# One-hot operands laid out token by token, and key numbers picked in bf16, in a two-layer encoder with product-key experts

## What is computed

```
def one(x):                                   # x: 128 tokens of RMSNorm(x)
    q = (x @ wq).reshape(C, 8 heads, 2, 128)
    s = einsum('chpk,hpnk->chpn', q, sub_keys)           # scores of 128 keys, two halves
    top_s, top_i = top_k(s, 16)
    cand = top_s[:, :, 0, :, None] + top_s[:, :, 1, None, :]
    best_s, best_j = top_k(cand.reshape(C, 8, 256), 16)
    i1 = take_along_axis(top_i[:, :, 0], best_j // 16)   # key number of the first half
    i2 = take_along_axis(top_i[:, :, 1], best_j % 16)    # key number of the second half
    e = i1 * 128 + i2
    g = softmax(best_s)
    h = gelu(einsum('cd,chkd->chk', x, expert_u[e]))
    return einsum('chk,chkd->cd', g * h, expert_v[e])
```

## Time and profile before

| | us |
|---|---|
| median of 3 runs | 3570.25 |
| the runs | 3565.03, 3570.25, 4163.93 |
| the profiled execution, its own time | 3574.14 |
| span of the profiled execution | 3572.3 |
| mean granted clock of PE, share of full | 0.972 |

### The profile page before, as it was taken

How to read it: one execution, slowest core, us unless ns; L and a number is a source line. 1 busy time by engine, 2 the same in 40 slices (tenths; PEclk the granted TensorE clock), 3 DMA queues, 4 the chain that set the end, 5 groups by cost and what they waited for, 6 DMA issues and landing times.

```text
span 3572.3 us, 55663 instructions
## 1 busy us (share of the span) xinstructions
PE 3347.4 (94%) x17714; PEld 2967.7 (83%) x17714; DVE 2547.1 (71%) x4795; ACT 1246.7 (35%) x2013; POOL 1161.9 (33%) x647
## 2 busy tenths in 40 slices
PE   7999998699879999999999999986998799999999
PEld 6787798699868888888877878886998688888888
DVE  4544699888688676676645547998886877676676
ACT  4433332233333333333344423222332333333332
POOL 3444344101233333333144443441112333333331
PEclk9999999899989999999999999998999899999999
DMA  3111343477788888888521123435677888888885
GB/s 120 65 53 65 107 132 110 165 260 269 283 304 318 310 302 307 304 297 304 202 101 65 53 77 110 126 115 178 247 273 282 303 319 306 309 300 303 298 305 205
DMA packets 235870, 763.87 MB, mean 214 GB/s; under 512 B 19056, under 2 KB 117488, under 8 KB 200688
## 3 DMA queue, kind: packets, MB, share of 16 engines
q1 hardware_dynamic: 198896, 494.09, 39.7%
q0 software_dynamic: 36864, 268.45, 21.8%
HBM read 684.87 MB, written 77.59 MB: 213 GB/s over the span
## 4 chain that ended last, share of the span: by engine, by line
PE 67%; DVE 15%; DVEq 6%; issue 6%; DMA 3%; ACT 1%; POOL 1%; SPq 0%; ACTq 0%; POOLq 0%
PE PS L417 19%; PE PS L419 19%; PE PS L418 19%; PE PS L691 6%; DVE EQ L1268 2%; PE PS L584 1%; DVEq L1277 1%; DVEq L1315 1%; DVE I L1221 1%; DVE I L1228 1%; DMA VRAW<-in_peer_v 1%; DVE SW L1222 1%; POOL RL L1418 1%; PE PS L578 1%; DVE EQ L1272 1%
## 5 line engine op out<-in xcount | busy, mean ns | idle before, releaser
L1418 POOL TENSOR_TENSOR RL<-RAW,RH 128x1024 fp32r<-128x1024 f32 x320 | 801.8, 2515 | 824.2 <-ACT RH L763 823.9
L417 PE MATMUL PS<-XH,RH 128*128 128x384 f32 (+1 forms) x2720 | 985.5, 362 | 21.6 <-ACT GEL L950 21.6
L419 PE MATMUL PS<-XH,RL 128*128 128x384 f32 (+1 forms) x2720 | 957.8, 352 | 0.0
L418 PE MATMUL PS<-XL,RH 128*128 128x384 f32 (+1 forms) x2720 | 956.5, 352 | 0.0
L1452 POOL DMA_INDIRECT ROWS<-in_peer_rows,LIST x256 | 292.0, 1141 | 1449.2 <-DVE X L1316 1405.2
L417 PE MATMUL PS<-VHI,WHI 128*128 128x512 f32 x1536 | 601.9, 392 | 40.9 <-DVE WLO L1375 40.9
L419 PE MATMUL PS<-VHI,WLO 128*128 128x512 f32 x1536 | 600.1, 391 | 0.0
L418 PE MATMUL PS<-VLO,WHI 128*128 128x512 f32 x1536 | 600.1, 391 | 0.0
L1372 DVE TENSOR_TENSOR VLO<-VRAW,VHI 128x1024 fp32r<-128x1024 f32 x256 | 321.6, 1256 | 340.2 <-ACT VHI L958 340.2
L417 PEld LDWEIGHTS PS<-XH,RH 128*128 128x128 f32 x2720 | 520.8, 191 | 50.9 <-issue 22.9
L418 PEld LDWEIGHTS PS<-XL,RH 128*128 128x128 f32 x2720 | 518.6, 191 | 28.3
(11 more groups left out here) (228 smaller groups left out, 3454.3 us busy)
## 6 DMA issues: line engine op xcount, KB each, us to landing
RAW<-in_peer_u SPq DMA_DIRECT2D x256, 512.0 KB, 5.6
VRAW<-in_peer_v SPq DMA_DIRECT2D x256, 512.0 KB, 5.6
RAW<-in_stream SPq DMA_DIRECT2D x128, 512.0 KB, 3.3
route_dram<-STAGE SPq DMA_DIRECT2D x16, 3072.0 KB, 10.1
GC<-route_dram SPq DMA_DIRECT2D x64, 768.0 KB, 8.7
gelu_dram<-GS SPq DMA_DIRECT2D x128, 192.0 KB, 3.6
GB<-gelu_dram SPq DMA_DIRECT2D x32, 768.0 KB, 10.0
ROWS<-in_peer_rows,LIST POOLq DMA_INDIRECT x256, 6.9
```

The source lines that it names most:

```text
L417: pe.matmul(acc, sh, mh, start=first, stop=False)
L418: pe.matmul(acc, sh, ml, start=False, stop=False)
L419: return pe.matmul(acc, sl, mh, start=False, stop=last)
L1418: pool.tensor_tensor(RL[:, k % 4, :], RAW[:, k % 2, :], RH[:, k % 4, :].bitcast(F32), ALU.subtract).then_inc(S.low_part, 1)
```

## The change

Picking the key numbers: F16, JF, J8 and the compare table EQ become bf16, with the token tile innermost (4 adjacent values). One compare of 2048 elements takes the place of the eight, one product of 2048 the place of the two, and four sums of halves (1024, 512, 256 and 128 outputs, the last one in float32 to I12) that of the two reductions, with a drain after each. The casts at lines 1246 and 1255 now write with the token tile innermost. Every value is a whole number under 128.

One-hot operands: OA, OE and OB become [8 tokens, 128], so a one-hot vector is contiguous. IT holds each value twice, and the operands are written as [8, 64, 2], with the pair from IT read again 64 times. They are still five operations of 1024 elements. REST, OA and OE move to other addresses.

```
-        IOTA4 = sb("IOTA4", [P, P, 4], BF16)
+        IOTA4 = sb("IOTA4", [P, TOPK, TT], BF16)
+        IOTAB = sb("IOTAB", [P, P], BF16)
-        EQ = at("EQ", 22 * K, [P, TT, TOPK, TOPK])
-        EQ2 = at("EQ2", 26 * K, [P, TT, TOPK, TOPK])
+        EQ = at("EQ", 22 * K, [P, 2, TOPK, TOPK, TT], BF16)
+        EQS = at("EQS", 26 * K, [P, 2, TOPK, 8, TT], BF16)
-        F16 = at("F16", 31 * K, [P, TT, 2, TOPK])
+        F16 = at("F16", 31 * K, [P, 2, TOPK, TT], BF16)
-        JF = at("JF", 32 * K + 512, [P, 2, TT, TOPK])
-        J8 = at("J8", 42 * K, [P, TT, TOPK])
+        JF = at("JF", 32 * K + 512, [P, 2, TOPK, TT], BF16)
+        J8 = at("J8", 42 * K, [P, TOPK, TT], BF16)
+        I12 = at("I12", 38 * K, [P, 2, TT, P])
-        IT = at("IT", 48 * K, [P, 5, SD], BF16)
+        IT = at("IT", 48 * K, [P, 5, SD, 2], BF16)
-        OA = at("OA", 55 * K, [P, 2, 2, P, 4], BF16)
-        OE = at("OE", 59 * K, [P, 2, P, 4], BF16)
-        OB = at("OB", 61 * K, [P, 2, 3, 2, P, 4], BF16)
+        OA = at("OA", 56 * K, [P, 2, 8, P], BF16)
+        OE = at("OE", 73 * K, [P, 8, P], BF16)
+        OB = at("OB", 61 * K, [P, 2, 3, 8, P], BF16)
...
-                                    m = pe.matmul(PS[:, 4 + g % 2, t * P:(t + 1) * P], OA[:, g // 2 % 2, g % 2, :, t],
-                                                  OB[:, g // 2 % 2, p, g % 2, :, t], start=p == 0, stop=p == 2)
+                                    m = pe.matmul(PS[:, 4 + g % 2, t * P:(t + 1) * P], OA[:, g // 2 % 2, g % 2 * 4 + t, :],
+                                                  OB[:, g // 2 % 2, p, g % 2 * 4 + t, :], start=p == 0, stop=p == 2)
...
-                        dve.tensor_copy(F16[:], I16[:])
+                        dve.tensor_copy(F16[:].rearrange("p h r t -> p t h r"), I16[:])
...
-                        dve.tensor_copy(JF[:], JHL[:])
+                        dve.tensor_copy(JF[:].rearrange("p h j t -> p h t j"), JHL[:])
...
-                        ramp = IOTA[:, 0:TOPK].unsqueeze(1).to_broadcast([P, TOPK, TOPK])
-                        for half, (e, dst) in enumerate(((EQ, I1), (EQ2, I2))):
-                            for t in range(TT):
-                                dve.tensor_tensor(e[:, t], JF[:, half, t, :].unsqueeze(2).to_broadcast([P, TOPK, TOPK]),
-                                                  ramp, ALU.is_equal)
+                        rows = EQ[:].rearrange("p h j r t -> p (h j) r t")
+                        dve.tensor_tensor(rows, JF[:].rearrange("p h j t -> p (h j) t").unsqueeze(2).to_broadcast(
+                            [P, 2 * TOPK, TOPK, TT]), IOTA4[:].unsqueeze(1).to_broadcast([P, 2 * TOPK, TOPK, TT]),
+                            ALU.is_equal)
                         dve.drain()
-                        for half, e in enumerate((EQ, EQ2)):
-                            dve.tensor_tensor(e[:], e[:], F16[:, :, half, :].unsqueeze(2).to_broadcast([P, TT, TOPK, TOPK]),
-                                              ALU.mult)
+                        flat = EQ[:].rearrange("p h j r t -> p h j (r t)")
+                        dve.tensor_tensor(flat, flat, F16[:].rearrange("p h r t -> p h (r t)").unsqueeze(2).to_broadcast(
+                            [P, 2, TOPK, TOPK * TT]), ALU.mult)
                         dve.drain()
-                        for e, dst in ((EQ, I1), (EQ2, I2)):
-                            dve.tensor_reduce(dst[:, :, bass.ds((2 * i + head) * TOPK, TOPK)], e[:], AX, ALU.add)
+                        sums = EQS[:].rearrange("p h j r t -> p (h j) r t")
+                        dve.tensor_tensor(sums, rows[:, :, 0:8, :], rows[:, :, 8:16, :], ALU.add)
+                        dve.drain()
+                        for n in (4, 2):
+                            dve.tensor_tensor(sums[:, :, 0:n, :], sums[:, :, 0:n, :], sums[:, :, n:2 * n, :], ALU.add)
+                            dve.drain()
+                        dve.tensor_tensor(I12[:, :, :, bass.ds((2 * i + head) * TOPK, TOPK)].rearrange("p h t j -> p h j t"),
+                                          EQS[:, :, :, 0, :], EQS[:, :, :, 1, :], ALU.add)
                         dve.drain()
...
-                    dve.tensor_copy(IT[:, n, :] if n < 2 else REST[:, 0, :], PS[:, n, 0:SD])
+                    if n < 2:
+                        dve.tensor_copy(IT[:, n], PS[:, n, 0:SD].unsqueeze(2).to_broadcast([P, SD, 2]))
+                    else:
+                        dve.tensor_copy(REST[:, 0, :], PS[:, n, 0:SD])
...
-                    dve.tensor_copy(IT[:, 2 + p, :], REST[:, p % 2, :])
+                    dve.tensor_copy(IT[:, 2 + p], REST[:, p % 2, :].unsqueeze(2).to_broadcast([P, SD, 2]))
...
-                            return IT[:, row, bass.ds(8 * n, 8)].rearrange("p (g t) -> p g t", g=2).unsqueeze(
-                                2).to_broadcast([P, 2, P, 4])
-
-                        numbers = IOTA4[:].unsqueeze(1).to_broadcast([P, 2, P, 4])
+                            return IT[:, row, bass.ds(8 * n, 8), :].unsqueeze(2).to_broadcast([P, 8, P // 2, 2])
+
+                        def tokens(tile):
+
+                            return tile.rearrange("p t (i d) -> p t i d", d=2)
+
+                        numbers = IOTAB[:].rearrange("p (i d) -> p i d", d=2).unsqueeze(1).to_broadcast([P, 8, P // 2, 2])
-                        dve.tensor_tensor(OA[:, slot], numbers, of_tokens(0), ALU.is_equal)
-                        dve.tensor_tensor(OE[:], numbers, of_tokens(1), ALU.is_equal)
+                        dve.tensor_tensor(tokens(OA[:, slot]), numbers, of_tokens(0), ALU.is_equal)
+                        dve.tensor_tensor(tokens(OE[:]), numbers, of_tokens(1), ALU.is_equal)
                         dve.drain()
                         for p in range(3):
-                            m = dve.tensor_tensor(OB[:, slot, p], OE[:], of_tokens(2 + p), ALU.mult)
+                            m = dve.tensor_tensor(tokens(OB[:, slot, p]), tokens(OE[:]), of_tokens(2 + p), ALU.mult)
```

More of the change, by code:

```diff
@@ L204, in program @@
         BS = at("BS", 37 * K, [P, TT * PH])
-        I1 = at("I1", 38 * K, [P, TT, P])
-        I2 = at("I2", 40 * K, [P, TT, P])
+        I12 = at("I12", 38 * K, [P, 2, TT, P])
+        I1, I2 = I12[:, 0], I12[:, 1]
         STAGE = [at(f"STAGE{s}", 24 * K * s, [P, NK, TB]) for s in range(2)]
-        IT = at("IT", 48 * K, [P, 5, SD], BF16)
-        REST = at("REST", 52 * K, [P, 2, SD])
-        OA = at("OA", 55 * K, [P, 2, 2, P, 4], BF16)
-        OE = at("OE", 59 * K, [P, 2, P, 4], BF16)
-        OB = at("OB", 61 * K, [P, 2, 3, 2, P, 4], BF16)
+        IT = at("IT", 48 * K, [P, 5, SD, 2], BF16)
+        REST = at("REST", 75 * K, [P, 2, SD])
+        OA = at("OA", 56 * K, [P, 2, 8, P], BF16)
+        OE = at("OE", 73 * K, [P, 8, P], BF16)
+        OB = at("OB", 61 * K, [P, 2, 3, 8, P], BF16)
         VRAW = at("VRAW", 0, [P, 2, D])
@@ L1000, in _ @@
             dve.wait_ge(iota_made, 1)
-            dve.tensor_copy(IOTA4[:], IOTA[:].unsqueeze(2).to_broadcast([P, P, 4]))
+            dve.tensor_copy(IOTA4[:], IOTA[:, 0:TOPK].unsqueeze(2).to_broadcast([P, TOPK, TT]))
+            dve.tensor_copy(IOTAB[:], IOTA[:])
             dve.wait_ge(const_in, 64)
@@ L1293, in _ @@
                     dve.wait_ge(S.choice_transposed, count(l, "choice_transposed", n + 1))
-                    dve.tensor_copy(IT[:, n, :] if n < 2 else REST[:, 0, :], PS[:, n, 0:SD])
+                    if n < 2:
+                        dve.tensor_copy(IT[:, n], PS[:, n, 0:SD].unsqueeze(2).to_broadcast([P, SD, 2]))
+                    else:
+                        dve.tensor_copy(REST[:, 0, :], PS[:, n, 0:SD])
                 dve.drain()
                 for p in range(3):
-                    dve.tensor_copy(IT[:, 2 + p, :], REST[:, p % 2, :])
+                    dve.tensor_copy(IT[:, 2 + p], REST[:, p % 2, :].unsqueeze(2).to_broadcast([P, SD, 2]))
                     dve.drain()
                     if p < 2:
-                        dve.tensor_tensor(REST[:, (p + 1) % 2, :], REST[:, p % 2, :], IT[:, 2 + p, :], ALU.subtract)
+                        dve.tensor_tensor(REST[:, (p + 1) % 2, :], REST[:, p % 2, :], IT[:, 2 + p, :, 0], ALU.subtract)
                         dve.drain()
```

## The result

The changed kernel takes 3509.4 us (median of 4 runs, 3508.6 to 3510.4) against 3570.4 for the kernel before, a ratio of 0.983 (95% interval 0.981 to 0.984): 61 us less. The forecast was 3527, in a range of 3494 to 3560. The profiled execution took 3508.56 us with a span of 3506.7, against 3572.3. One run of the kernel before, at 4163.93 us, was slow and is left out of the ratio.

The account below looks back on a forecast made before the run. DVE was taken to bound the query stage, with routing balanced between DVE and PE. 3574.1 - 46 (pick) + 3 (turn) = 3531 us profiled; the runs' median lies 3.9 lower, so 3527, range 3494 to 3560.

Parts of the forecast that it names:

- What bounds the query stage: Query stage: DVE leads at 32.5 us per head, becoming 29.6, a hair above PE's 29.5.
- PE's wait at the end of the stage: Query stage end: 27 us minus what DVE gains, some 23 us in a layer, so it hides nothing.
- The pick, 2.9 us per head: Query stage, DVE, undisturbed: 7.9 us removed, 4.7 added, 0.3 for small edits; 16 heads give 46 us.
- small edits: Pick: casts to F16 and JF and the last sum write with jumps, 0.1 us each taken, 0.3 per head.
- Collisions, left at nothing with 18 us either way: Pick: POOL low parts stall two-input DVE instructions; 4 us saving left out, 2.2 us in every other head as range.
- Turn, +3 us: Between query and routing stages: IT twice as wide lengthens copies and casts, 1.4 us per layer, 3 us in all.
- DVE's one-hot operations at 687 ns: Routing stage: five instructions of 1024 bf16 elements keep their time though the inner run shrinks from four values to two.
- the rival: Routing stage: one-hot operands lose the paired rate, 1225 ns instead of 687, +240 us, 3767 us; chance 0.11.
- the estimate was 3680 us: Routing stage: by the skill page's rule on hopping at every word, one-hot instructions cost +0.35 us each.
- I take contiguity to bring PE nothing: Routing stage, PE: the weight load sets 108 ns per pair, and contiguous one-hot vectors leave it unchanged.
- the first rival: Routing stage: PE loads contiguous one-hot vectors faster, DVE then binds, 17 us gained, 3510 us; chance 0.27.
- 1.07 us of gaps that it counted as slack: Routing stage, DVE: three longer gaps, 0.17 + 0.20 + 0.70 us over the usual, put DVE's own pace at 33.7 us per round.

Follow-up runs that it names:

- both experiments on collisions: Changed kernel with two reductions replacing the pick's four sums: 3498.0 us; changed kernel with POOL writing 8 of 1024 columns per query-stage low part: 3489.7 us.
- the reductions: Changed kernel with the pick's four sums of halves replaced by two reductions over the 16 ranks: 3498.0 us, ratio 0.979.

## Why the prediction was right or wrong

- **What bounds the query stage** (DVE, down to PE's 29.5 us per head): right. DVE leads in the changed kernel's chain, and both experiments on collisions ran into PE. What it says of PE's wait at the end of the stage (27 us minus what DVE gains) was wrong: by the 27 us gained nothing would have been left, and 15.11 us were. It took PE's own end of the stage as fixed, but PE had lost 10 us in waits for DVE within the stage and ended 13.5 us earlier. That the margin held is luck: by the prediction's own sum it would have been used up.
- **The pick, 2.9 us per head:** right for the untouched part: 4.7 us, small edits 0.1 each.
- **Collisions, left at nothing with 18 us either way:** mis-sized, by 10 us. By mean against undisturbed time the pick lost 54 us before (Rows 3, 4) and loses 37 after, 33 at L1277 and 4 at L1273. The steps ahead of the pick lost about 25 us before and 32 after (L1243 16 x (0.83 - 0.23) = 10, L1263 16 x (1.22 - 0.19) = 16, two others 6). Two of those before, at 226 and 219 ns undisturbed:

```profile
L1256 DVE TENSOR_TENSOR BV<-B 128x64 f32 x16 | 8.0, 500 | 0.0
L1246 DVE CAST F<-I 128x128 f32<-128x128 uint32 x16 | 7.9, 493 | 0.0
```

So 79 us became 69, and 46 + 10 is the 57 measured, to within 1. All 16 heads have a collision at L1277, 12 at L1243, 8 at L1263. Before, the most that one place had was 17 of the 128 compares and 8 of the 32 products: they had offered POOL several places. The period of DVE's heads and that of PE's blocks, on which ACT's and POOL's parts follow, are now 29.4 and 29.5 us, so each head meets POOL at the same place. That it is this lock is argued from the times. With the reductions, which don't stand still, the collisions went to L1263 (10 of 16 heads), L1245 (7) and L1248 (5), at an unchanged 29.4 us per head, which fits it; no run shifted POOL's work against DVE's and left the rest alone.
- **Turn, +3 us:** +2.1. The copies cost what was priced, 0.395 and 0.20 us each, 1.4 us in a layer; a third of a microsecond of it fell into a wait for PE's transposes.
- **DVE's one-hot operations at 687 ns:** right, and the rival had a true mechanism at a run of one. The rule of the Trainium skill ("Vector Engine (DVE) Microarchitecture Reference", 5.2) against runs of one 4-byte word, by which the estimate was 3680 us, didn't show here, where the word is read again in place: 687 ns. What its section 5.1 has, that rows of two 16-bit elements still run paired, did.
- **"I take contiguity to bring PE nothing": this step failed.** The runs showed in its place that the hops of the moving operand set the pace: 108 ns per pair at 8 bytes, 53 contiguous. The inference that the load sets it, from 0.11 against 0.15 us per pair at 96 and 128 weight columns, rests on a misreading. The row of 0.59 us in Rows 11 begins with a load that went ahead while a product of 512 columns was still streaming. By the matmuls of the same two groups, in the kernel before, there is no difference:

```profile
157.47 0.60 PE L578 MATMUL PS<-IDN,PR 128*128 128x128 f32 x4
```

```profile
164.85 0.60 PE L548 MATMUL PS<-IDN,QSL 128*96 128x128 f32 x4
```

Less the last one's 0.27 us both are 0.33 / 3 = 0.11 us per pair. The contiguous load of 114 ns that I set beside OA's 108 was float32, and no run says which operand sets the pace there, so it said nothing of a bf16 stream. The rule that I quoted from the Trainium skill ("SBUF — State Buffer", "Door 1: The DMA port swizzle"), that two hits on a line of 16 bytes are enough for full speed, has two on a line at 8 bytes. The pace there was 108 ns, so for the moving operand it is refuted; the 54 ns came with 4 bytes. Nor was the weight path slow, which the Trainium skill ("TensorE: Matmul & The Clock Gate", "Weight-path perf modes") has fast for such weights: with OA hopping 8 bytes and OB contiguous a pair took 54 ns.
- **What the first rival was worth:** its 17 us came out as 14.8. It said DVE's pace would bind, and it does; but of the 1.07 us of gaps that it counted as slack only the one of 0.92 was a wait for ACT. The others are DVE's own, and a round went from 34.8 to 34.3, not 33.7. By the starts of OA, the first seven rounds of both layers gained 9.2 us. Behind the last OB of a layer PE now starts its last one-hot product after 3.1 us instead of 6.3 and 6.1, since it no longer runs behind DVE: 6.2 us more. With 0.6 lost on the way to WF that is the 14.8. The 17 us were thus near by luck: the slack was counted too large and the end of the stage not at all.

So the time came 18 us under the forecast: 11 from the query stage, 15 from routing, 1 from the turn, less the 4 of the rest and 5 of the profiled executions' places among their runs' medians. It stayed within the range because the lower end had been drawn from just these two, the first rival's 3510 and fewer collisions; the forecast itself had neither.

## What to carry to other kernels

The two operands of a matmul didn't bear the same hop here: before laying one out for the vector engine's sake, time a stream with that hop, of that type. An inference from float32 rows didn't carry to bf16, and a pace is read from starts, not from the length of a merged row. Where two engines' periods come close, as here, a collision can fall in every turn at the same instruction, so look at the longest and the median of a group, not only at its mean. And before taking out a stall, work out the pace of the engine that is late next: here of the 8 x 2.05 = 16 us that a layer lost at the sum, only 4.2 were there to be had.

## What the hardware showed beyond that

- A bf16 moving operand of 128 columns: 53 ns per pair at 2 bytes from element to element, 54 at 4, 108 at 8, 216 at 16 (at 4 and 16 with the stationary operand at the same hop). The stationary operand at 8 bytes adds 1 ns to 53. What it is in the read of the moving operand that doubles with the hop, no run says.
- A DVE operation with two SBUF inputs stands still in bf16 as it does in float32 while POOL writes a low part (2743 for 693 ns); tensor_reduce of the same tile doesn't (1224 ns at most). One input alone doesn't save an operation: a cast from SBUF to SBUF (L1246 of the kernel before) took up to 2417 ns for 219 beside a low part.
- With PE waiting 3 us at the start of a round, its granted clock in the stage went from 0.99 to 0.91, and the 12 matmuls after that wait took 751.27 - 750.07 = 1.20 us, 100 ns each, at a granted clock of 0.50 (750.10 to 751.20 us), the level of 1.2 GHz. The faster stream left PE idle and the clock took part of it back, at no cost that the rounds show, since DVE leads (PE's busy share is 83% of the stage).
